# A rotary embedding without its permutation on TensorE: sines by source row, and partner rows added by DMA

## The reference

```python
def rope_partial(t, cos, sin):
    half = ROPE_DIM // 2          # 8
    ...
    t1 = t[..., :half]
    t2 = t[..., half:ROPE_DIM]
    return jnp.concatenate([t1 * c - t2 * s, t2 * c + t1 * s, t[..., ROPE_DIM:]], axis=-1)
...
        dq = rope_partial(dq.reshape(B, S, DIFF_HEADS, 2, DIFF_DH), cos, sin)
        dk = rope_partial(dk.reshape(B, S, DIFF_HEADS, 2, DIFF_DH), cos, sin)
...
        s1 = jnp.einsum('bhqd,bhkd->bhqk', q1b, k1, ...) * scale_d
        s2 = jnp.einsum('bhqd,bhkd->bhqk', q2b, k2, ...) * scale_d
        p = (softmax(where(chunk_mask, s1, NEG)) - lam * softmax(where(chunk_mask, s2, NEG)))
        od = jnp.einsum('bhqk,bhkd->bhqd', p, dv_t)
```

## Time and profile before

| | |
|---|---|
| Time, median of three runs | 2474.12 us (2471.16, 2474.12, 2476.0) |
| Span of the profiled execution | 2471.1 us; its own time is not listed apart from the three runs |
| TensorE busy | 2432.9 us, 98% of the span, 11654 records |
| VectorE, ScalarE, GpSimd busy | 70%, 41%, 42% |
| Granted TensorE clock | full in all 40 slices, as tenths |
| DMA | mean 70 GB/s; GpSimd's own queue 2.5% of 16 engines |

### The profile page before, as it was taken

One profiled execution on the slowest core, in us unless ns is written; L12 is line 12 of the kernel. 1 busy time (PEld: TensorE's weight loads), 2 busy tenths in 40 slices (PEclk: granted clock), 3 DMA queues, 4 the chain that ended last, 5 costly groups with the idle time before them and its releaser, 6 DMA issues.

```text
span 2471.1 us, 31309 instructions
## 1 busy us (share of the span) xinstructions
PE 2432.9 (98%) x11654; PEld 1998.7 (81%) x11654; DVE 1724.5 (70%) x2391; ACT 1022.3 (41%) x1740; POOL 1029.1 (42%) x714
## 2 busy tenths in 40 slices
PE   9999999999999999999999999999999999999998
PEld 7777788888778888888887878887878888888887
DVE  6777757673696666666679966777397666666676
ACT  6454656562542222222246436555262232323233
POOL 4666542211534444444455553331343343434343
PEclk9999999999999999999999999999999999999999
DMA  4211221132111111111122852222211111111122
GB/s 162 77 55 48 87 60 44 55 117 77 47 43 56 56 51 52 52 52 52 55 60 111 188 129 69 58 74 98 78 40 56 47 56 47 57 46 60 43 61 102
DMA packets 157125, 171.77 MB, mean 70 GB/s; under 512 B 11184, under 2 KB 114352, under 8 KB 156848
## 3 DMA queue, kind: packets, MB, share of 16 engines
q1 hardware_dynamic: 153376, 157.46, 20.7%
q0 software_dynamic: 3168, 11.54, 2.5%
q10 hardware_dynamic: 432, 0.79, 0.1%
HBM read 124.13 MB, written 15.20 MB: 56 GB/s over the span
## 4 chain that ended last, share of the span: by engine, by line
PE 86%; DVE 6%; ACT 3%; POOL 2%; issue 2%; DMA 1%; SPq 0%; POOLq 0%; DVEq 0%; ACTq 0%
PE PS L1638 24%; PE PS L1643 24%; PE PS L1640 24%; PE PS L1736 3%; PE PS L1723 2%; PE PS L1757 2%; PE PS L1754 2%; PE PS L1717 2%; PE PS L1720 1%; DVE R0f L2043 0%; PE PS L1722 0%; DVE Pb L1942 0%; DVE Pb L1940 0%; DMA stage<-scr_mix 0%; DVE sm L1928 0%
## 5 line engine op out<-in xcount | busy, mean ns | idle before, releaser
L1638 PE MATMUL PS<-R,wh 128*128 128x512 f32 x2952 | 1165.7, 395 | 8.6 <-DVE stage L2031 2.6
L1643 PE MATMUL PS<-R,wh 128*128 128x512 f32 x2952 | 1152.2, 390 | 2.7 <-DVE R L2076 2.0
L2480 POOL TENSOR_TENSOR lows<-values,wh 128x512 fp32r<-128x512 f32 (+1 forms) x416 | 604.6, 1455 | 1050.7 <-ACT wh L2228 938.8
L1640 PE MATMUL PS<-R,lows 128*128 128x512 f32 x2512 | 980.3, 390 | 1.1 <-POOL lows L2480 1.0
L1643 PEld LDWEIGHTS PS<-R,wh 128*128 128x128 f32 x2952 | 554.5, 188 | 124.2 <-DVE R L2076 3.8
L1638 PEld LDWEIGHTS PS<-R,wh 128*128 128x128 f32 x2952 | 555.4, 188 | 120.5 <-issue 3.6
L2228 ACT ACTIVATE wh<-values 128x512 fp32r<-128x512 f32 (+1 forms) x417 | 259.9, 623 | 719.2 <-PE PS L1643 707.1
L1640 PEld LDWEIGHTS PS<-R,lows 128*128 128x128 f32 x2512 | 472.4, 188 | 93.4 <-issue 3.6
L2056 DVE TENSOR_TENSOR X<-PS,X 128x512 f32<-128x512 f32 x400 | 271.5, 689 | 200.1 <-PE PS L1643 199.1
L2480 POOL TENSOR_TENSOR late_r<-late,wh 128x512 fp32r<-128x512 f32 x83 | 122.5, 1476 | 134.9 <-ACT wh L2228 94.2
L1640 PE MATMUL PS<-R,late_r 128*128 128x512 f32 x440 | 171.2, 389 | 0.0
(11 more groups left out here) (276 smaller groups left out, 2791.3 us busy)
## 6 DMA issues: line engine op xcount, KB each, us to landing
values<-w_ff_dram SPq DMA_DIRECT2D x94, 256.0 KB, 2.7
values<-w_in_dram SPq DMA_DIRECT2D x88, 256.0 KB, 2.7
R<-R SPq DMA_DIRECT2D x96, 128.0 KB, 2.3
X<-X POOLq DMA_DIRECT2D x22, 512.0 KB, 5.8
values<-w_up_dram SPq DMA_DIRECT2D x38, 256.0 KB, 2.9
values<-w_gate_dram SPq DMA_DIRECT2D x36, 256.0 KB, 2.9
late<-w_ff_dram SPq DMA_DIRECT2D x36, 256.0 KB, 2.9
values<-w_down_dram SPq DMA_DIRECT2D x32, 256.0 KB, 2.7
```

The lines of the kernel that those rows point to most:

```text
L1638: e.matmul(PS[:, b, :], wh, high, start=s["start"], stop=False)
L1640: e.matmul(PS[:, b, :], wl, high, start=False, stop=False)
L1643: m = e.matmul(PS[:, b, :], wh, low, start=False, stop=s["stop"])
L2480: e.tensor_tensor(T.wl[piece.v][:, 0:m], T.wv[piece.v][:, 0:m], T.wh[:, piece.h, 0:m].bitcast(F), ALU.subtract).then_inc(*sg.up("w_lo", pi ...
```

## The change

The sine table is now indexed by the source row and has its signs swapped accordingly: DVE multiplies the stage tile itself, in SBUF, by it. GpSimd multiplies the tile by the cosines as before, but only after the sine multiply, since both read the same tile and the cosines overwrite it. Then GpSimd issues four DMAs of 8 partitions x 512 columns (16 KB) each, which add the product's rows 8 to 15 to the tile's rows 0 to 7 and the other way round, and the same for 64 to 79. ScalarE's and GpSimd's splits wait for the fourth. Two semaphores, `rot0` and `rot1`, take turns, and a rotation is issued only once the one before it on the same semaphore has been rounded (`qk_hi`). The permutation's matmul, its PSUM bank, its table and the load of it are gone. The planner sees the new steps and lays out all engines anew.

```diff
             def rotate(half, i, which=which, split=split):
-                b, given = self.side_bank()
                 j, gj = self.next_stage()
                 key = (u.name, which, half)
-                self.step("rotate", key=key, half=half, i=i, j=j, gj=gj, b=b, given=given)
-                self.step("rotate_add", key=key, i=i, j=j)
-                self.bank_given[b] = [("rot_sin", key)]
-                self.stage_given[j] = [("rot", key)]
-                u.rotated = ("rot", key)
-                split(half, i)
+                self.step("rotate", key=key, half=half, i=i, j=j, gj=gj)
+                turned = f"rot{self.rotations % 2}"
+                self.rotations += 1
+                self.step("rotate_add", key=key, i=i, j=j, turned=turned, given=self.turned_before[turned])
+                self.turned_before[turned] = [("qk_hi", key)]
+                self.stage_given[j] = [(turned, key)]
+                u.rotated = (turned, key)
+                split(half, i, (turned, key))
...
-        elif kind == "rotate":
-            for event in s["given"]:
-                w.wait_ge(*sg.at(*event))
-            w.wait_ge(*sg.at("evac", s["key"]))
-            w.wait_ge(*sg.at("perm", 0))
-            e.matmul(PS[:, s["b"], :], T.perm[:, :], T.stage[s["i"]], start=True, stop=True).then_inc(*sg.up("permuted", s["key"]))
...
             w.wait_ge(*sg.at("table", 0))
-            w.wait_ge(*sg.at("permuted", s["key"]))
-            e.tensor_tensor(stage[s["j"]], PS[:, s["b"], :], T.TABF[:, 1, cols(s["half"])], ALU.mult).then_inc(*sg.up("rot_sin", s["key"]))
+            w.wait_ge(*sg.at("evac", s["key"]))
+            e.tensor_tensor(stage[s["j"]], stage[s["i"]], T.TABF[:, 1, cols(s["half"])], ALU.mult).then_inc(*sg.up("rot_sin", s["key"]))
...
             w.wait_ge(*sg.at("table", 0))
-            w.wait_ge(*sg.at("permuted", key))
+            w.wait_ge(*sg.at("rot_sin", key))
             e.tensor_tensor(st, st, T.TABF[:, 0, cols(s["half"])], ALU.mult).then_inc(*sg.up("rot_cos", key))
         elif kind == "rotate_add":
-            key, st = s["key"], stage[s["i"]]
+            key, st, part = s["key"], stage[s["i"]], stage[s["j"]]
+            for event in s["given"]:
+                w.wait_ge(*sg.at(*event))
             w.wait_ge(*sg.at("rot_cos", key))
-            w.wait_ge(*sg.at("rot_sin", key))
-            e.tensor_tensor(st, st, stage[s["j"]], ALU.add).then_inc(*sg.up("rot", key))
+            for n, o in enumerate((0, 8, 64, 72)):
+                across = slice(o ^ 8, (o ^ 8) + 8)
+                e.dma_start(st[o:o + 8, :], part[across, :], accum_op=ALU.add).then_inc(*sg.up(s["turned"], key if n == 3 else (key, n), by=16))
...
-            c[o + j, C_SIN:C_SIN + S] = -sin[j]
-            c[o + j + 8, C_SIN:C_SIN + S] = sin[j]
+            c[o + j, C_SIN:C_SIN + S] = sin[j]
+            c[o + j + 8, C_SIN:C_SIN + S] = -sin[j]
```

More of the change, by code:

```diff
@@ L25 @@
 NV = 129
-C_ID, C_PERM, C_COS, C_SIN, C_SEL, C_MASK = 0, 128, 256, 1280, 2304, 3328
+C_ID, C_COS, C_SIN, C_SEL, C_MASK = 0, 128, 1152, 2176, 3200
 NC = C_MASK + 3 * 512
@@ L175, in __init__ @@
         self.ones = self.new("ones", [128, 128], F, 512)
-        self.perm = self.new("perm", [128, 128], F, 512)
         self.maskb = self.new("maskb", [128, 128], BF, 256)
@@ L282, in __init__ @@
         self.on_slot = {}
+        self.rotations, self.turned_before = 0, dict(rot0=[], rot1=[])
     def step(self, kind, **what):
@@ L681, in project, with split @@
         for which in range(3):
-            def split(half, i, which=which):
+            def split(half, i, rotated=None, which=which):
                 names = [f"ql0{half}", f"ql1{half}"] if which == 0 else [f"kh0{half}", f"kh1{half}"]
@@ L686, in split @@
                 self.step("split_qk", u=u, which=which, half=half, i=i, freed=list(freed), prev=[prev.qk_done] if prev else [],
-                          st=("rot", (u.name, which, half)) if u.kind == DIFF else ("evac", (u.name, which, half)),
+                          st=rotated if u.kind == DIFF else ("evac", (u.name, which, half)),
                           slots=[(name, self.on_slot[name]) for name in names if name in self.on_slot])
@@ L2549, in sync_program @@
             e.dma_start(T.ident[:, :], cst[:, C_ID:C_ID + 128]).then_inc(*sg.up("ident", 0, by=16))
-            e.dma_start(T.perm[:, :], cst[:, C_PERM:C_PERM + 128]).then_inc(*sg.up("perm", 0, by=16))
         elif kind == "x_load":
@@ L2815, in constants @@
         for j in range(8):
-            c[o + j + 8, C_PERM + o + j] = 1.0
-            c[o + j, C_PERM + o + j + 8] = 1.0
             c[o + j, C_COS:C_COS + S] = cos[j]
             c[o + j + 8, C_COS:C_COS + S] = cos[j]
-            c[o + j, C_SIN:C_SIN + S] = -sin[j]
-            c[o + j + 8, C_SIN:C_SIN + S] = sin[j]
+            c[o + j, C_SIN:C_SIN + S] = sin[j]
+            c[o + j + 8, C_SIN:C_SIN + S] = -sin[j]
     for h in range(8):
```

## The result

| | median us | runs |
|---|---|---|
| before, in the same comparison | 2472.64 | 2470.98 to 2476.0, 4 runs |
| the change | 2518.3 | 2514.78 to 2520.78, 4 runs |
| ratio | 1.018 | 95% interval 1.0167 to 1.0193 |

The change makes the kernel slower by 45.7 us; no change was forecast, and 2518 lies outside the range. The profiled execution's span grew from 2471.1 to 2514.6 us, +43.5.

What follows compares the result with a forecast made beforehand. TensorE (PE busy 98%) was taken as the bound, except a0's attention, bound by softmax through DVE. First scores +14.9, a0 to a3 0, +1.4, -5.8, -11.4: -0.9 us on 2474.1 gives 2473 us; range 2462 to 2486.

Steps and rivals of the forecast that it cites:

- the waits inside the new order: Attention unit a0, last eight jobs without triples (three TensorE matmuls each): kept at 37.9 us, a change of 0.
- a1 and a2 follow TensorE's work: Attention units a1 and a2: lengths scaled from TensorE's rows, 72.8 to 74.2 and 70.1 to 64.3 us.
- GpSimd has the room for its four extra rotations' worth in a1 and a2: GpSimd in a1 and a2: busy 46.3 of 72.8 and 43.1 of 70.2 us, so 8.6 more each fits.
- The clock was assumed full: Attention units a0 to a3: TensorE's time taken from the earlier trace's start-to-start distances, without a term for a lower clock.
- The permutation's size, -13.9 us: TensorE, first 240 us: each of 16 permutations costs it 0.87 us, 13.9 us in all.
- its smaller work: Attention units a2 and a3: less TensorE work shortens them by 5.8 and 11.4 us.
- GpSimd's issues: GpSimd's queue: four DMA issues of 0.86 us, 3.44 us a rotation, 2.15 more than before, 34 us over 16.
- The landing: The accumulating 16 KB DMAs: land in 2.5 us, bounded by 2.3 and 7.7; the sum does not turn on it.
- The path to a0's scores: Before a0's first scores: TensorE waits 2.5 and 4.8 us for weight pieces 15 and 16; scores at 92.5, 14.9 later.
- The sine: DVE's sine multiply, now reading SBUF: 2 us more in all over 16 instructions, 0.3 us of it in a0.
- Rival 2: GpSimd's queue before the first scores: slower issues bound it, 2479.6 to 2486 us, deciding from 1.15 us an issue; chance 0.26.
- The last sentence of the prediction: DVE mid-softmax: an instruction waiting for an addition's semaphore would be a cost, put at nothing.

Runs made afterwards that it cites:

- f2: e1's work (addition on GpSimd, no exchange of rows, no DMA) planned as if it had the four DMAs, in the changed kernel's order: 2507.0 us, +35.5 against before.
- h5: e1 in its own order, with four accumulating DMAs behind each addition into a tile nobody reads: 2504.9 us, +30.9 against before.
- f4: The change, same order, with matmuls on ones put into TensorE's two longest waits: 2512.9 us, +41.4 against before.
- g2: e4 in the same order, with each permutation's matmul cut to 2 columns in place of 512: 2474.6 us, +2.6 against before.
- e1: The change with one addition on GpSimd in place of the four DMAs, no exchange of rows, planned anew: 2470.2 us, -3.7 against before.
- e4: The kernel before, permutation kept, but DVE's sine multiply reads the stage tile in SBUF; no exchange of rows, planned anew: 2475.6 us, +1.7 against before.

## Why the prediction was wrong

- **The step that failed: the waits inside the new order were put at nothing.** The prediction added up TensorE's rows for the new order, kept a0 at 37.9 us ("what is taken from TensorE here is idle") and let a1 and a2 follow TensorE's work, 74.2 and 64.3: together 176.4. The change took 47.5, 88.2 and 73.3, together 209.0. f2 has this order without a single DMA and took 205.3. So 28.9 of the 32.6 us by which these three units exceed the forecast are there without the DMAs. I had seen that the new order has no triples between a0's last eight jobs, and costed it at nothing.
- **"GpSimd has the room for its four extra rotations' worth in a1 and a2": wrong too, and the smaller error in this order.** The DMAs add 10.2 us to f2. In the order of the addition they add 42.5, and h5 has 34.6 us for 54 us of issues. A busy share was no measure of room, since the queue is strictly ordered and its splits hold the stage buffers, for which VectorE's evacuations wait, and TensorE for these.
- **The clock was assumed full**, as the rows of before had it (0.98 to 1.00 in these units). No term of the sum was there for idle time that slows what follows. a0 to a2 of the change have 0.86, 0.90 and 0.95. f4, with work put into two waits, is 4.3 us faster, at the edge of what can be told.
- **The permutation's size, -13.9 us: right as TensorE's time, wrong as the kernel's.** g2 gives back nothing of it in the old order, and e1 3.7 us in a new one. I read PE's 98% as "a cut in TensorE's work pays unless another wait takes its place", and in a2 and a3 I let its smaller work, moved triples included, pay in full (-17 us). In a3, at a clock of 1.00, it nearly did (42.1 for 39.4). In a2 it did not.
- **GpSimd's issues: right, 3.44 us a rotation forecast, 3.2 to 4.7 measured.** The landing was near: 2.5 against 2.9.
- **The path to a0's scores was right by luck.** Forecast: waits of 2.5 and 4.8 us for low parts, and the transposes of the values reached at 73.4. TensorE reached them at 61.4, since in its order they stand 12 us earlier than where I put them, and waited 8.8 us there. The sum came close (95.4 for 92.5), and f2, without the DMAs that were to cause those waits, starts its scores at 93.6.
- **The sine: 2 us forecast; e4 is 1.7 above before, in an order of its own, not told from nothing.** In the change its median rose from 0.681 to 1.146 us with a longest of 3.5. These rows agree with the rule of the Trainium skill ("SBUF — State Buffer", Who interferes with whom) that the prediction cited, that a DVE instruction with two SBUF inputs contends with a GpSimd instruction that reads SBUF. No large loss came of it.
- Rival 2 had the sign, and GpSimd's queue as the culprit, which is part of it, but the wrong place and a condition (issues over 1.15 us) that was not met: the issues take 0.81. No rival had the order itself as the cost. The last sentence of the prediction, on a VectorE instruction that waits for an addition in the middle of a softmax, came near one form of the loss: an evacuation by VectorE that waits for a copy, before a0's attention.

No version tried beats the kernel before. e1, which leaves the exchange out, is 3.7 us faster: that is what any free way of exchanging the rows could bring in the orders tried here.

## What to carry to other kernels

A busy share of 98% says that an engine has little idle time, not that time taken from it comes back: in a schedule balanced by a planner, take the work away by itself first (here 2 columns in place of 512, same order) and see. Ask who waits for an engine's queue before calling an issue on it cheap: in the order of the addition, 48 small DMAs of 0.81 us, 39 us in all, cost 37. And when a planner lays out the order anew, measure the order apart from the edit: plan the old work by the new costs, and the other way round.

## What was unexpected of the hardware

- The granted clock of the changed kernel falls with a wait of TensorE and is still low when it is busy again: 0.57 and 0.74 in two stretches of 10 us that follow each other, the second one fully busy.
- VectorE and GpSimd slow each other. Two rows of VectorE, of the changed kernel, beside GpSimd's multiply, DMA issues and low part from 51.1 to 60.8 us:

```profile
54.09 1.82 DVE L1885 TENSOR_SCALAR Pb<-Pb,vec 128x1024 f32<-128x1024 f32 x1
55.83 1.49 DVE L1794 TENSOR_TENSOR sm<-sm 128x1 f32<-128x1 f32 x1
```

  Before, the first took 0.74 us, and the second, one column, 0.14. In f2, where GpSimd issues no DMA there but multiplies and adds, they took 1.78 and 1.24. The Trainium skill ("SBUF — State Buffer", Who interferes with whom) states that a DVE instruction with two SBUF inputs contends with a GpSimd instruction that reads SBUF. The second row, which has two SBUF inputs, agrees: at ten times its length it has more likely waited than worked. Which instruction of GpSimd held it was not tested.
- An accumulating DMA of 8 rows is issued in 0.81 us, nearly as long as one of 128 rows (0.86), but lands in 2.9 us against 5.8.
